# Level operands ahead of the split, and chunk pairs in the HGRN phases, in a two-layer hybrid trunk

## The chip, the cores and the metric

The kernel runs on one core of a Trainium2 chip. The metric is the device time of one execution in microseconds (us); lower is better. TensorE (PE) multiplies, VectorE (DVE) and ScalarE (ACT) prepare its operands, SyncE (SP) issues the weight loads. Each engine works its own queue in order and waits on semaphores.

## The reference

```python
def hgrn2_mixer(xn, w_in, lb, out_gain, w_out):
    q, fr, v, g = jnp.split(xn @ w_in, 4, axis=-1)            # 2048 columns each
    q = silu(q) * 128 ** -0.5
    f = lb + (1 - lb) * sigmoid(fr); k = 1 - f
    o = chunked_gated_recurrence(heads(q), heads(k), heads(v), heads(log(f)))
    return (rms_norm(o, out_gain) * silu(g)) @ w_out

def conv_glu_ffn(xn, w_up, conv_w, w_down):
    gate, val = jnp.split(causal_dwconv(xn @ w_up, conv_w), 2, axis=-1)
    return (silu(gate) * val) @ w_down

h = h + hgrn2_mixer(rms_norm(h, ..), ..);       h = h + conv_glu_ffn(rms_norm(h, ..), ..)
h = h + short_conv_mixer(rms_norm(h, ..), ..);  h = h + conv_glu_ffn(rms_norm(h, ..), ..)
return rms_norm(h, final_norm)
```

The sequence has 256 tokens, the model 2048 features, the HGRN mixer 16 heads of 128, the feed-forward part 5632 features. All is float32.

## The kernel before

**Chunks.** All weights are streamed once, in 816 chunks of 512 KB, through a ring of four slots (RING). Of each float32 operand two parts are kept, a high part in the type of the fast matmul and the low rest, and a product is made of high times high, high times low and low times high. For every chunk ACT copies the weights to their high part (`hi_ready`, L324), DVE subtracts to get the low part (`lo_ready`, the split, L537), and PE does 8 matmuls of 512 columns with the high part (`feature_highs`, L1035, "highs", H below) and 8 of 256 columns with the low part (`feature_lows`, L1045, "lows", L). PE adds to `hi_used` after the highs and to `lo_used` after the lows. ACT refills a slot's high part after `hi_used` of the chunk that was in it, and DVE's split for chunk c+4, which stands in DVE's step for chunk c, waits for `lo_used` of chunk c. SP loads raw weights once the split of the slot's last chunk is done.

**Phases.** HGRN_IN has 4 blocks (i) of 4 heads, each with 4 groups (g) of 8 chunks: forget gate, q, v (g = V_GROUP = 2) and output gate. HGRN_OUT is the output projection of the mixer, 32 chunks. Then follow UP0, DOWN0, SC_IN, SC_OUT, UP1 and DOWN1. In group 2 the roles are turned: `token_boths` (512 columns, both parts of the weights, L1058) comes first and needs `lo_ready` too, and `token_highs` (L1067) comes second and frees the high part. `run` in PE's `phase_of` says how many chunks' highs go before their lows: 1 in HGRN_IN, HGRN_OUT and DOWN1 (H L H L), RUN = 2 elsewhere (H H L L, a pair).

**Levels.** The recurrence of four heads is worked out over 128 tokens at a time by levels 1, 2, 4, ..., 128 (LEVELS). Counted from the start of group 2, n is the number of the chunk (0 to 15 in groups 2 and 3). PLAN says after which chunk's PE work a stage is issued: the diagonal (m = -1) after n = 2, levels m = 0 to 7 after 3, 5, 6, 8, 10, 12, 13 and 15, and the output stage (twelve matmuls, L1175) after 18, which is chunk 2 of the next block's first group, or of HGRN_OUT. A level stage is four matmuls of 128 columns (L1196, eight in the trace); it reads `ql` and `kl`, which DVE's `level_operands` writes two chunks ahead, into buffer m % 2, and writes `side`, of which there are two (STAGES). DVE then merges `side` into `a_diag` (`take_stage`, a copy under a mask, L806) and adds to `stage_free`, without which PE doesn't start the stage after the next. `prefixes` (L786) updates the running products between two levels.

**DVE's order in a step.** In `phase_of` of DVE a step is: `ahead` (here `last_take`), the split, the correction of a finished half group (`corrected`, L570 or L565), then `hgrn`: take of the stage after n - 1, `prefixes`, the work of `output_steps` for the block before, `level_operands`. A level's take has no wait of its own: the split of its step waits for `lo_used` of chunk n, which PE gives after the stage.

**The output of a block.** `output_steps` of DVE, step 2: the gate product (L829), the copy of the output stage (L797), the gain (L833, four); step 3, behind the split of that step: the high and low part of `act` (L838, L840), which adds to `act_ready`. In HGRN_OUT the chunks of the first group come in the order (part, k) = (0,0) (0,1) (1,0) (0,2) (1,1) (0,3) (1,2) (1,3), and the first chunk with a new k waits for `act_ready` of block k. The last block's `act` is made in HGRN_OUT itself, in steps 2 and 3, and chunk 5, (0,3), is the first that needs it. After chunk 6 comes a stage that sums squares (L1027), for which DVE waits in the same step (`rms`).

Below, o0 to o31 are the chunks of HGRN_OUT, v0 to v7 those of group 2 of a block; H(o5) is the 8 highs of o5, L(o5) its lows, "the split for o6" the DVE operation that makes its low part.

Of the kernel before, what the change touches and what calls it, by code (L numbers as in the profile page):

```python
# [44 lines left out]
RUN = 2  # L45
LEVELS = [1, 2, 4, 8, 16, 32, 64, 128]
# [36 lines left out]
HGRN_IN = Phase(None, 4, 4, DT, scales=3)  # L83
HGRN_OUT = Phase(HGRN_IN, 2, 2, DT)
# [24 lines left out]
LEAD = 2  # L109
# [21 lines left out]
def trunk(nc, x, parameters, hgrn_w_in, hgrn_w_out, sc_w_in, sc_w_out, ffn_w_up, ffn_w_down, final_norm, identity,  # L131
          level_masks, out):
    with ExitStack() as ctx:
# [3 lines left out]
        def sem(name):  # L137
            return ctx.enter_context(nc.semaphore(name))
# [70 lines left out]
        scaled_ready = sem("scaled_ready")  # L209
        stage_done = sem("stage_done")  # L210
        stage_free = sem("stage_free")
        inits = sem("inits")
        chain = sem("chain")
        late_chain = sem("late_chain")
# [36 lines left out]
        def at(i, per, first):  # L251

            return i * per + first
# [238 lines left out]
        def _(dve):  # L492
# [287 lines left out]
            def prefixes(i, m):  # L780

                n = LEVELS[m]
                pre = halves(fpre[:], n)
                shape = [P, TG * T // (2 * n), n]
                await_mark(i)
                mark(v.tensor_tensor(pre[:, :, 1], pre[:, :, 1], pre[:, :, 0, n - 1:n].to_broadcast(shape), ALU.mult))  # L786
# [67 lines left out]
            def hgrn(i, first, g, kk):  # L854
                n = g * HGRN_IN.cpg + kk - 2 * HGRN_IN.cpg
                if first and (g, kk) == (0, X_LATE_AT):
                    input_low_parts(X_LATE)
                    lower_bound()
                if first and (g, kk) == (0, BOUND_AT):
                    lower_bound_rest()  # L860
                if first and g == 0 and kk in SQUARES_AT:
                    n_sq = SQUARES_AT.index(kk)
                    dve.wait_ge(sq_ready, n_sq + 1)
                    src = [ta, tb][n_sq % 2]
                    then(v.tensor_tensor(sq_acc[:], sq_acc[:], src[:, 0:2, :], ALU.add))
                    then(v.tensor_tensor(sq_acc[:], sq_acc[:], src[:, 2:4, :], ALU.add))
                    if n_sq == DT // TG - 1:
                        then(v.tensor_copy(sq_mirror[:], mirrored(sq_acc[:, :, P:])))
                    v.sem_inc(sq_sum, 1)
                if first and (g, kk) == (0, last):  # L870
                    rms(0, S_RS_HGRN, T + 2)
                for stage, (after, _, _) in enumerate(PLAN):
                    if n == after + 1:
                        take_stage(i, stage)
                if kk == last and g != V_GROUP:
                    scaled(i, HGRN_IN, g, min(g, V_GROUP), ta[:])
                if first and (g, kk) == (1, 0):
                    dve.wait_ge(inits, 4)
                    dve.wait_ge(masks_loaded, 16)
                    dve.wait_ge(conv_par_loaded, 16)  # L880
                if (g, kk) == (1, 0):

                    dve.wait_ge(gate_sig, at(i, 3, 1))
                    for j in range(TG):
                        c = bass.ds(i * TG + j, 1)
                        o = v.tensor_scalar(fpre[:, j, :], tb[:, j, :], one_less_lb[:, c], lb[:, c], ALU.mult, ALU.add)
                    link(o, i)
                    v.tensor_scalar(kh[:], fpre[:], -1.0, 1.0, ALU.mult, ALU.add)
                    v.tensor_scalar(kl[:, 1], mirrored(fpre[:, :, P:]), -1.0, 1.0, ALU.mult, ALU.add)
                for after, what, m in PLAN:  # L890
                    if what == LEVEL and 0 <= m < len(LEVELS) - 1 and n == after - LEAD + 1:
                        prefixes(i, m)
                if not first:
                    output_steps(i - 1, g, kk)
                if n == 0:

                    dve.wait_ge(gate_sig, at(i, 3, 2))
                    v.scalar_tensor_tensor(out=qh[:], in0=ta[:], scalar=float(P) ** -0.5, in1=tb[:],
                                           op0=ALU.mult, op1=ALU.mult).then_inc(qk_ready, 1)
                    dve.wait_ge(qk_ready, at(i, 1 + len(LEVELS), 1))  # L900
                for after, what, m in PLAN:
                    if what == LEVEL and m >= 0 and n == after - LEAD:
                        level_operands(i, m)

            phase_of(HGRN_IN, hgrn, ahead=last_take, into=lambda g: ta)
            late[0] += 4 * HGRN_IN.n
            carried.append(lambda g, kk: output_steps(HGRN_IN.n - 1, g, kk))
            residual_phase(HGRN_OUT, 0, 8, NORM_FFN, 1, S_RS_OUT)
# [95 lines left out]
        def _(pe):  # L1004
# [94 lines left out]
            def phase_of(phase, src, ready, ready0, per=1, rs=None, pieces=None, carry=None, rs_at=(0, RS_AT)):  # L1099

                def between(i, first, g, kk):
                    if carry and first:
                        carry(g, kk)
                    if first and rs and (g, kk) == rs_at:
                        sum_squares(*rs)
                    if pieces:
                        pieces(i, first, g, kk)

                def body(i, first):
                    for g in range(phase.groups):  # L1110
                        seen = 0
                        steps = phase.steps(first, g)
                        run = 1 if phase in (HGRN_IN, HGRN_OUT, DOWN1) else RUN
                        ends_here = phase is DOWN1 and i == DOWN1.n - 1 and g == DOWN1.groups - 1
                        for k0 in range(0, phase.cpg - RING * ends_here, run):
                            chunks = []
                            for kk in range(k0, k0 + run):
                                part, k, begin, end = steps[kk]
                                c = phase.c0 + g * phase.cpg + kk
                                a = g * phase.parts + part  # L1120
                                if begin:

                                    pe.wait_ge(acc_free, at(i, phase.api, phase.a0 + a + 1))
                                need = k + 1 if phase.parts == 2 else k * KC // TG + 1
                                if first and g == 0 and need > seen:
                                    pe.wait_ge(ready, ready0 + need * per)
                                    seen = need
                                pe.wait_ge(hi_ready, at(i, phase.cpi, c + 1))
                                to = acc[:, a % SETS]
                                if phase is DOWN1:  # L1130
                                    pe.wait_ge(lo_ready, at(i, phase.cpi, c + 1 + RING))
                                    low, high = wide_tokens(to, c, src, k, begin, end)
                                    low.then_inc(lo_used, 1)
                                    high.then_inc(hi_used, 1)
                                elif phase is HGRN_IN and g == V_GROUP:
                                    if first and part == 0:
                                        pe.wait_ge(mirror_ready, k + 1)
                                    pe.wait_ge(lo_ready, at(i, phase.cpi, c + 1 + RING))
                                    token_boths(to, c, src, k, begin)
                                else:  # L1140
                                    feature_highs(to, c, src, k, begin)
                                chunks.append((c, to, k, end))
                            if phase is DOWN1:
                                between(i, first, g, k0)
                                continue
                            for kk in range(k0, k0 + run - 1):
                                between(i, first, g, kk)
                            for c, to, k, end in chunks:
                                if phase is HGRN_IN and g == V_GROUP:
                                    token_highs(to, c, src, k, end)  # L1150
                                else:
                                    pe.wait_ge(lo_ready, at(i, phase.cpi, c + 1 + RING))
                                    feature_lows(to, c, src, k, end)
                            between(i, first, g, k0 + run - 1)
                        if ends_here:
                            last_chunks(acc[:, g % SETS], CHUNKS - RING, src, steps[-RING:])
                loop(pe, phase, body)
# [88 lines left out]
```

## Time and profile before

| | |
|---|---|
| median of 3 runs | 2348.74 us (2348.08 to 2348.83) |
| the profiled execution | 2348.23 us |
| its span, first to last instruction | 2346.4 us |
| granted TensorE clock, mean | 0.999 of full speed |
| PE busy | 2326.7 us (99%) |
| DVE busy | 1698.7 us (72%) |
| ACT busy | 1047.0 us (45%) |
| DMA | 434.91 MB, 185 GB/s |

The kernel before is bound by TensorE from 9.10 us to 2338.7 us. Busy time of matmuls overlaps in the records, so that the time of a stretch is read from the starts of its rows. HGRN_IN ends at 418.10 us, HGRN_OUT at 512.04 us.

### The profile page before, as it was taken

The page shows a single profiled execution, that of the slowest core. Times are in us where ns is not written, and L with a number is a line of the kernel's source. Part 1 is how long each engine was busy: PE and PEld are TensorE (multiplying, and loading weights), DVE is VectorE, ACT ScalarE, POOL GpSimd, SP SyncE. Part 2 cuts the span into 40 slices and gives each one's busy share as a digit, 9 for nine tenths or more (in the row PEclk, how much of TensorE's full clock was granted, in tenths as well). Part 3 has the DMA queues.
Part 4 walks back from the last instruction along what each step waited for, and adds up shares of the span by engine and source line. Part 5 has one row for each costly group of instructions (what it writes and reads, how often), then busy time and mean ns, then how long its engine had stood idle before and what let it go on. Part 6 is the DMA issues. An engine that isn't in the chain of part 4 may idle for free.

```text
span 2346.4 us, 37237 instructions
## 1 busy us (share of the span) xinstructions
PE 2326.7 (99%) x13180; PEld 2045.2 (87%) x13180; DVE 1698.7 (72%) x2151; ACT 1047.0 (45%) x1146; POOL 2.7 (0%) x8
## 2 busy tenths in 40 slices
PE   8999999999999999999999999999999999999998
PEld 7888888888888888888888888888888888888887
DVE  7979788778788878865555666666788788785444
ACT  6443444454444444444444444444444444443443
POOL 0000000000000000000000000000000000000000
PEclk9999999999999999999999999999999999999999
DMA  7555555556666566566555666565656656665664
GB/s 245 160 171 153 170 164 167 170 179 190 188 187 190 185 188 188 187 196 190 189 187 187 192 188 189 180 197 179 198 180 192 194 179 195 188 206 185 192 192 157
DMA packets 410283, 434.91 MB, mean 185 GB/s; under 512 B 13264, under 2 KB 386384, under 8 KB 410064
## 3 DMA queue, kind: packets, MB, share of 16 engines
q1 hardware_dynamic: 409616, 431.53, 58.9%
q10 hardware_dynamic: 576, 2.16, 0.3%
q8 instruction: 58, 0.95, 0.2%
q14 instruction: 33, 0.27, 0.0%
HBM read 431.54 MB, written 2.10 MB: 185 GB/s over the span
## 4 chain that ended last, share of the span: by engine, by line
PE 97%; DVE 2%; issue 1%; ACT 0%; DMA 0%; DVEq 0%; ACTq 0%
PE acc L1035 54%; PE acc L1045 28%; PE acc L1081 3%; PE acc L1082 3%; PE acc L1080 3%; PE acc L1058 2%; PE side L1196 1%; PE acc L1067 1%; PE side L1175 0%; PE side L1191 0%; DVE kl L769 0%; DVE a_diag L806 0%; DVE a_diag L800 0%; DMA par<-in_parameters 0%; PE side L1027 0%
## 5 line engine op out<-in xcount | busy, mean ns | idle before, releaser
L537 DVE TENSOR_TENSOR w_parts<-raw,w_parts 128x1024 fp32r<-128x1024 f32 x816 | 982.5, 1223 | 575.9 <-PE acc L1045 347.9
L324 ACT ACTIVATE w_parts<-raw 128x1024 fp32r<-128x1024 f32 x816 | 859.3, 1060 | 1023.3 <-PE acc L1035 804.5
L1035 PE MATMUL acc<-xn,w_parts 128*128 128x512 f32 x4352 | 1051.1, 392 | 9.1 <-DVE xn L595 9.1
L1035 PEld LDWEIGHTS acc<-xn,w_parts 128*128 128x128 f32 x4352 | 797.6, 189 | 161.6 <-issue 9.1
L1045 PEld LDWEIGHTS acc<-xn,w_parts 128*128 128x128 f32 x4352 | 565.1, 191 | 25.2
L1045 PE MATMUL acc<-xn,w_parts 128*128 128x256 f32 x4352 | 573.2, 283 | 0.0
L1035 PE MATMUL acc<-act,w_parts 128*128 128x512 f32 x1216 | 293.6, 391 | 0.7 <-DVE act L840 0.7
L1035 PEld LDWEIGHTS acc<-act,w_parts 128*128 128x128 f32 x1216 | 222.5, 188 | 43.3 <-DVE act L840 0.9
L1045 PEld LDWEIGHTS acc<-act,w_parts 128*128 128x128 f32 x1216 | 158.0, 191 | 7.2
L1045 PE MATMUL acc<-act,w_parts 128*128 128x256 f32 x1216 | 160.2, 283 | 0.0
L1080 PE MATMUL acc<-w_parts,act 128*128 128x512 f32 x352 | 137.3, 390 | 0.0
L1082 PE MATMUL acc<-w_parts,act 128*128 128x512 f32 x352 | 137.0, 389 | 0.0
L1081 PE MATMUL acc<-w_parts,act 128*128 128x512 f32 x352 | 137.0, 389 | 0.0
L338 ACT ACTIVATE corr<-acc 128x512 f32<-128x512 f32 x144 | 85.7, 595 | 76.0 <-PE acc L1045 76.0
L619 DVE SCALAR_TENSOR_TENSOR tb<-pad,par,tb 128x256 f32<-128x256 f32 x208 | 90.9, 482 | 12.2 <-DVE tb L617 0.3
L619 DVE SCALAR_TENSOR_TENSOR ta<-pad,par,ta 128x256 f32<-128x256 f32 x176 | 77.5, 482 | 11.9
L1082 PEld LDWEIGHTS acc<-w_parts,act 128*128 128x128 f32 x352 | 66.1, 188 | 13.7
L1080 PEld LDWEIGHTS acc<-w_parts,act 128*128 128x128 f32 x352 | 66.1, 188 | 13.6
L1081 PEld LDWEIGHTS acc<-w_parts,act 128*128 128x128 f32 x352 | 66.1, 188 | 13.5
L570 DVE TENSOR_TENSOR pad<-acc,corr 128x512 f32<-128x512 f32 x96 | 65.6, 684 | 0.0
L367 ACT ACTIVATE xn<-h,par 128x256 fp32r<-128x256 f32 x64 | 28.7, 501 | 77.0 <-DVE h L657 59.8
L399 ACT ACTIVATE ta<-ta 128x1024 f32<-128x1024 f32 x22 | 23.4, 1065 | 82.7 <-DVE ta L619 82.7
(123 smaller groups left out, 1014.9 us busy)
## 6 DMA issues: line engine op xcount, KB each, us to landing
raw<-in_ffn_w_up SPq DMA_DIRECT2D x352, 512.0 KB, 3.6
raw<-in_ffn_w_down SPq DMA_DIRECT2D x176, 512.0 KB, 4.6
raw<-in_hgrn_w_in SPq DMA_DIRECT2D x128, 512.0 KB, 3.7
raw<-in_sc_w_in SPq DMA_DIRECT2D x96, 512.0 KB, 4.6
raw<-in_hgrn_w_out SPq DMA_DIRECT2D x32, 512.0 KB, 3.9
raw<-in_sc_w_out SPq DMA_DIRECT2D x32, 512.0 KB, 4.4
h<-in_x SPq DMA_DIRECT2D x4, 512.0 KB, 7.5
final_w<-in_final_norm ACTq DMA_DIRECT2D x1, 1024.0 KB, 7.0
```

What stands on the lines that cost most here:

```text
L324: nc.scalar.activation(w_parts[:, c % RING, :, 0, :], raw[:, c % RING], ACT.Copy).then_inc(hi_ready, 1)
L338: o = nc.scalar.activation(corr[:], acc[:, a % SETS, :, T:], ACT.Copy)
L367: o = nc.scalar.activation(xn[:, bass.ds(tile + j, 1), 0, :], h[:, bass.ds(tile + j, 1), :], ACT.Copy, scale=par[:, bass.ds(weight + tile ...
L537: v.tensor_tensor(w_parts[:, c % RING, :, 1, :], raw[:, c % RING], w_parts[:, c % RING, :, 0, :].bitcast(F32), ALU.subtract).then_inc(lo_r ...
L570: o = v.tensor_tensor(dst[:, part * TW:(part + 1) * TW, :], acc[:, a % SETS, :, 0:T], corr[:], ALU.add)
L619: o = v.scalar_tensor_tensor(out=dst[:, j, :], in0=src, scalar=w, in1=dst[:, j, :], op0=ALU.mult, op1=ALU.add)
L1035: o = mm(to[:, j, :], w[:, q, 0, j * P:(j + 1) * P], src[:, k * KW + q, :, :].rearrange("p n t -> p (n t)"), start=begin and q == 0, stop= ...
L1045: o = mm(to[:, j, T:], w[:, q, 1, j * P:(j + 1) * P], src[:, k * KW + q, 0, :], start=False, stop=end and q == KW - 1, skip_group_check=True)
L1058: o = mm(to[:, b, :], x_block(src, k * KW + q, 0, b), w[:, q].rearrange("p n d -> p (n d)"), start=begin and q == 0, stop=False, skip_grou ...
L1080: mm(bank, x_hi, hi, start=begin and q == 0, stop=False)
L1081: low = mm(bank, x_hi, lo, start=False, stop=False)
L1082: high = mm(bank, x_lo, hi, start=False, stop=end and q == KC - 1)
```

## The change

Two things are changed. In HGRN_IN and HGRN_OUT `run` becomes RUN, so that these 160 chunks go in 80 pairs; a stage that follows an even chunk is then issued between the highs and the lows of its pair, one that follows an odd chunk after the pair. And DVE's level work (prefixes, level operands, take) moves from behind the split of its step to ahead of it (`levels`), with the operands ahead of the take; a step that takes a stage waits for `stage_done` of that stage first and adds to a new semaphore, `stage_seen`, for which nobody waits. The work of `output_steps` stays behind the split.

```diff
             def levels(i, g, kk):
+                last_take(i, g, kk)
+                n = g * HGRN_IN.cpg + kk - 2 * HGRN_IN.cpg
+                done = [stage for stage, (after, what, _) in enumerate(PLAN) if what == LEVEL and n == after + 1]
+                for stage in done:
+                    dve.wait_ge(stage_done, at(i, HGRN_STAGES, S_HGRN + stage + 1))
+                    v.sem_inc(stage_seen, 1)
+                for after, what, m in PLAN:
+                    if what == LEVEL and 0 <= m < len(LEVELS) - 1 and n == after - LEAD + 1:
+                        prefixes(i, m)
                 for after, what, m in PLAN:
                     if what == LEVEL and m >= 0 and n == after - LEAD:
                         level_operands(i, m)
+                for stage in done:
+                    take_stage(i, stage)
...
-                for stage, (after, _, _) in enumerate(PLAN):
-                    if n == after + 1:
-                        take_stage(i, stage)
...
-                for after, what, m in PLAN:
-                    if what == LEVEL and 0 <= m < len(LEVELS) - 1 and n == after - LEAD + 1:
-                        prefixes(i, m)
...
-            phase_of(HGRN_IN, hgrn, ahead=last_take, into=lambda g: ta)
+            phase_of(HGRN_IN, hgrn, ahead=levels, into=lambda g: ta)
...
-                        run = 1 if phase in (HGRN_IN, HGRN_OUT, DOWN1) else RUN
+                        run = 1 if phase is DOWN1 else RUN
```

Lines after the change are numbered one higher in DVE's part (the split is L538) and nine higher in PE's (highs L1044, lows L1054, the output stage L1184).

**Place 1, DVE in a block of the heads, step n = 4.** From the split of the step before the change (level 0 taken, prefixes of level 1, operands of level 2) to the next split:

```order
L537 TENSOR_TENSOR w_parts<-raw,w_parts 128x4x256 [waits lo_used,hi_ready]
L806 COPY_PREDICATED a_diag<-masks,side 128x512
L508 REGISTER_ALU
L786 TENSOR_TENSOR fpre<-fpre 128x256x2 [waits chain]
L508 REGISTER_ALU
L760 TENSOR_TENSOR ql<-qh,fpre 128x512 [waits chain]
L769 TENSOR_TENSOR kl<-kh,suf 128x64x4 x2
L775 REGISTER_ALU
L777 TENSOR_TENSOR suf<-suf,fpre 128x128x4 [waits qk_ready]
```

The same step after the change:

```order
L509 REGISTER_ALU [waits stage_done]
L787 TENSOR_TENSOR fpre<-fpre 128x256x2 [waits chain]
L509 REGISTER_ALU
L761 TENSOR_TENSOR ql<-qh,fpre 128x512 [waits chain]
L770 TENSOR_TENSOR kl<-kh,suf 128x64x4 x2
L776 REGISTER_ALU
L778 TENSOR_TENSOR suf<-suf,fpre 128x128x4 [waits qk_ready]
L807 COPY_PREDICATED a_diag<-masks,side 128x512
L536 REGISTER_ALU
L538 TENSOR_TENSOR w_parts<-raw,w_parts 128x4x256 [waits lo_used,hi_ready]
```

The split has moved from the first row to the last, and the take from ahead of the operands to behind them.

**Place 2, PE in HGRN_OUT, from o2 into the output stage.** Before the change the stage stands behind the lows of o2:

```order
L1035 MATMUL acc<-act,w_parts 128x512 [waits hi_ready,acc_free]
L1035 MATMUL acc<-act,w_parts 128x512 x7
L1045 MATMUL acc<-act,w_parts 128x256 [waits lo_ready]
L1045 MATMUL acc<-act,w_parts 128x256 x7
L1175 MATMUL side<-a_diag,vt 128x128 [waits stage_free,acc_free]
```

After the change it stands behind the highs of o2 and o3:

```order
L1044 MATMUL acc<-act,w_parts 128x512 [waits hi_ready,acc_free]
L1044 MATMUL acc<-act,w_parts 128x512 x7
L1044 MATMUL acc<-act,w_parts 128x512 [waits hi_ready,act_ready]
L1044 MATMUL acc<-act,w_parts 128x512 x7
L1184 MATMUL side<-a_diag,vt 128x128 [waits stage_free,acc_free]
```

The lows of o2, which release DVE's split in its step 2, have gone from ahead of the stage to behind it.

**Place 3, DVE in HGRN_OUT, steps 2 and 3, after the change.** The first row is the splits of steps 1 and 2 (for o5 and o6), the fifth that of step 3:

```order
L538 TENSOR_TENSOR w_parts<-raw,w_parts 128x4x256 [waits lo_used,hi_ready] x2
L830 TENSOR_TENSOR tb<-ta,tb 128x1024 [waits gate_sig]
L798 COPY o_sb<-side 128x1024 [waits stage_done,late_chain]
L834 SCALAR_TENSOR_TENSOR tb<-o_sb,par,tb 128x256 [waits stage_free]
L834 SCALAR_TENSOR_TENSOR tb<-o_sb,par,tb 128x256 x3
L538 TENSOR_TENSOR w_parts<-raw,w_parts 128x4x256 [waits lo_used,hi_ready,late_chain]
L839 CAST act<-tb 128x4x256
L841 TENSOR_TENSOR act<-tb,act 128x4x256 [waits late_chain]
```

Nothing has moved in this queue; it reads the same before the change, one line number lower.

**Place 4, PE in HGRN_OUT behind the output stage.** Before the change, from the highs of o4 to the first of o5:

```order
L1035 MATMUL acc<-act,w_parts 128x512 [waits hi_ready]
L1035 MATMUL acc<-act,w_parts 128x512 x7
L1045 MATMUL acc<-act,w_parts 128x256 [waits lo_ready]
L1045 MATMUL acc<-act,w_parts 128x256 x7
L1035 MATMUL acc<-act,w_parts 128x512 [waits hi_ready,act_ready]
```

After the change, the pair of o4 and o5:

```order
L1044 MATMUL acc<-act,w_parts 128x512 [waits hi_ready]
L1044 MATMUL acc<-act,w_parts 128x512 x7
L1044 MATMUL acc<-act,w_parts 128x512 [waits hi_ready,act_ready]
L1044 MATMUL acc<-act,w_parts 128x512 x7
L1054 MATMUL acc<-act,w_parts 128x256 [waits lo_ready]
```

The wait for `act_ready` of the last block now comes before the lows of o4.

## Rows read from the trace of the kernel before

**Rows 1.** The page, part 1: busy us (share of the span) and instructions.

```profile
PE 2326.7 (99%) x13180; PEld 2045.2 (87%) x13180; DVE 1698.7 (72%) x2151; ACT 1047.0 (45%) x1146; POOL 2.7 (0%) x8
```

**Rows 2.** Timeline of PE, single chunks, HGRN_OUT: start us, duration us, what.

```profile
445.00 2.00 PE L1035 MATMUL acc<-act,w_parts 128*128 128x512 f32 x8
...
509.24 2.00 PE L1035 MATMUL acc<-act,w_parts 128*128 128x512 f32 x8
```

**Rows 3.** Chain that ended last, pairs in UP0: start us, us, what.

```profile
535.33 3.65 PE acc L1035 x16
...
1064.17 3.65 PE acc L1035 x16
```

**Rows 4.** Timeline of PE, second block, v5 to v7 and two level stages.

```profile
178.38 0.28 PE L1067 MATMUL acc<-w_parts,xn 128*128 128x256 f32 x1
...
180.15 0.47 PE L1058 MATMUL acc<-w_parts,xn 128*128 128x512 f32 x1
...
182.08 0.28 PE L1067 MATMUL acc<-w_parts,xn 128*128 128x256 f32 x1
...
184.68 0.48 PE L1058 MATMUL acc<-w_parts,xn 128*128 128x512 f32 x1
```

**Rows 5.** Who waited for whom: us in total, times, longest us.

```profile
PE side L1196 <- DVE kl L769: 2.3, 4, 0.6
```

**Rows 6.** Timeline of DVE, second block, steps 3 and 4; idle in brackets.

```profile
174.14 1.23 DVE L537 TENSOR_TENSOR w_parts<-raw,w_parts 128x1024 fp32r<-128x1024 f32 x1 [2.59 <-ACT w_parts L324]
...
182.89 0.75 DVE L769 TENSOR_TENSOR kl<-kh,suf 128x256 f32<-128x256 f32 x2
```

**Rows 7.** Timeline of PE in HGRN_OUT: H(o2), output stage, H(o3), H(o4), H(o5), H(o6).

```profile
423.78 2.00 PE L1035 MATMUL acc<-act,w_parts 128*128 128x512 f32 x8
...
426.57 0.39 PE L1175 MATMUL side<-a_diag,vt 128*128 128x128 f32 x2
...
429.17 2.09 PE L1035 MATMUL acc<-act,w_parts 128*128 128x512 f32 x8
...
432.05 2.00 PE L1035 MATMUL acc<-act,w_parts 128*128 128x512 f32 x8
...
435.65 2.11 PE L1035 MATMUL acc<-act,w_parts 128*128 128x512 f32 x8 [0.65 <-DVE act L840]
...
438.55 2.00 PE L1035 MATMUL acc<-act,w_parts 128*128 128x512 f32 x8
```

**Rows 8.** Timeline of DVE in HGRN_OUT, steps 2 and 3.

```profile
426.97 1.23 DVE L537 TENSOR_TENSOR w_parts<-raw,w_parts 128x1024 fp32r<-128x1024 f32 x1 [1.57 <-ACT w_parts L324]
428.11 1.22 DVE L829 TENSOR_TENSOR tb<-ta,tb 128x1024 f32<-128x1024 f32 x1
429.52 1.22 DVE L797 COPY o_sb<-side 128x1024 f32<-128x1024 f32 x1 [0.19 <-PE side L1175]
...
432.51 1.22 DVE L537 TENSOR_TENSOR w_parts<-raw,w_parts 128x1024 fp32r<-128x1024 f32 x1
...
434.37 1.23 DVE L840 TENSOR_TENSOR act<-tb,act 128x1024 fp32r<-128x1024 f32 x1
```

**Rows 9.** Timeline of ACT in HGRN_OUT: the high parts for o12 to o15.

```profile
452.58 3.96 ACT L324 ACTIVATE w_parts<-raw 128x1024 fp32r<-128x1024 f32 x4
```

**Rows 10.** Timeline of PE, UP0: a pair with a squares stage between highs and lows.

```profile
528.74 3.83 PE L1035 MATMUL acc<-xn,w_parts 128*128 128x512 f32 x16
...
535.17 3.82 PE L1035 MATMUL acc<-xn,w_parts 128*128 128x512 f32 x16
```

**Rows 11.** Timeline of PE, the first two chunks of the kernel.

```profile
9.10 3.75 PE L1035 MATMUL acc<-xn,w_parts 128*128 128x512 f32 x8 [9.10 <-DVE xn L595]
...
14.29 2.01 PE L1035 MATMUL acc<-xn,w_parts 128*128 128x512 f32 x8
```

**Rows 12.** Windows at the end: busy PE, PEld, DVE, ACT, POOL, granted clock, DMA share, GB/s.

```profile
2338.00:2340.00 2.00, 0.74 (x4) 0.28 (x2) 0.69 (x1) 0.50 (x1) 0.00 (x0) 1.00 1.02 401
...
2342.00:2344.00 2.00, 0.00 (x0) 0.00 (x0) 0.04 (x1) 0.10 (x1) 0.00 (x0) 0.52 0.55 225
```

More of the change, by code:

```diff
@@ L211, in trunk @@
         stage_free = sem("stage_free")
+        stage_seen = sem("stage_seen")
         inits = sem("inits")
@@ L900, in hgrn, with levels @@
                     dve.wait_ge(qk_ready, at(i, 1 + len(LEVELS), 1))
+            def levels(i, g, kk):
+                last_take(i, g, kk)
[7 more added lines that the diff above has]
+                        prefixes(i, m)
                 for after, what, m in PLAN:
```

## Prediction

> **What bounds the kernel now.** I read the busy times first: PE is busy for 2326.7 of 2346.4 us, DVE for 1698.7 [rows 1]. The change can only pay where PE waits or where its own order costs time, and it does harm only where it makes PE wait. So I went on to the waits of PE, then to its timeline around each of them, and last to DVE's and ACT's timelines, to see who is late and by how much. Inside the two HGRN phases PE waits at two kinds of place. In every block of heads the stage of level 2 waits for `kl` from DVE, four times [rows 5]. And in HGRN_OUT H(o5) waits 0.65 us for the last block's `act` [rows 7].
>
> **Pairs.** From H(o8) at 445.00 to H(o31) at 509.24 PE does 23 single chunks, so one takes 2.793 us [rows 2]. In UP0 95 pairs lie between 535.33 and 1064.17, so a pair takes 5.567 us [rows 3]. A pair saves 2 x 2.793 - 5.567 = 0.019 us; 80 pairs save **1.5 us**. A chunk's highs take 1.84 and its lows 0.95 us; a pair's highs take 3.66.
>
> What pairs do to the stages: a stage after an even chunk now stands between highs and lows, 0.87 us later than before (3.66 against 2.79 from the start of the pair). Does it cost more there? In UP0 a pair with a squares stage in its middle takes 535.17 - 528.74 = 6.43 us, 0.86 over a plain pair [rows 10]; the same stage between single chunks takes 445.00 - 438.55 = 6.45 against 5.59, again 0.86 [rows 2, 7]. So the position costs nothing; for the 24 stages of the heads and outputs that move I take 0, with bounds of 0.05 us each to either side, 1.2 us in all.
>
> **Level operands.** In the second block the lows of v5 start at 178.38 and the next highs, one level stage later, at 180.15, in 1.77 us; from the lows of v6 to H(v7), with the stage of level 2, it is 184.68 - 182.08 = 2.60 [rows 4]. The wait costs 0.83 us, in four blocks **3.3 us**. Will it go? Before, DVE sits idle for 2.59 us until 174.14, when ACT's high part lets it split for v7, and `kl` of level 2 is ready at 182.89 + 0.75 = 183.64 [rows 6], 9.5 us later. Counted back from 178.38 (H 1.84, or 1.93 behind a stage, L 0.95, stage 0.81), H(v3) began at 169.97. With pairs H(v3) goes ahead of the diagonal stage, so the lows of v2, which in group 2 free the high part that ACT refills, start 0.89 later than they ended, at 170.86, and end at 171.8. ACT then needs 0.2 us to notice and 1.05, the split 1.14: DVE is free for step 3 at 174.2, as before. From there the queue to `kl` of level 2 is the same 9.5 us without one split (1.14) and one take (1.11), which now stand behind it: 7.25 us, ready at 181.45. PE wants the stage at 183.03 + 0.87 = 183.9. So the wait goes, with 2.4 us to spare. What is late next is the take of level 0, without which `side` isn't free for that stage: 181.45 + 0.61 + 1.11 = 183.2, 0.7 us early. Carried on step by step with the same durations the later stages are met with 0.8 us (level 6) to 2.9 us. The splits, now behind the level work, are up to 3 us later: that for v7 is done 8.7 + 4.4 = 13.1 us after H(v2), and PE needs it at 16.5. The new `stage_done` waits end when the stage does, which lies before DVE gets there in each step. All of that is covered by PE's ring of four.
>
> **The output of the last block.** This is where the change costs. Before, the split for o6 (DVE step 2) starts at 426.97, the gate product at 428.11, the copy of the output at 429.52, the split of step 3 at 432.51 and L840 at 434.37; it ends at 435.60, and H(o5) starts at 435.65 instead of 433.89 + 0.95 = 434.84 [rows 7, 8]. In that chain the split for o6 needed only L(o2), which PE had done ahead of the output stage. With pairs (place 2) PE does H(o2) from 423.78, H(o3) from 425.62, the output stage from 427.43, which takes 429.17 - 426.57 = 2.60 us, and L(o2) only from 430.03 to 431.1. DVE notices at 431.3. Its queue hasn't changed (place 3): the gate product, which needs nothing new, and the copy of an output that was done at 430 both stand behind the split. From the start of that split to the end of L840 are 435.60 - 426.97 = 8.63 us of back-to-back work, so `act_ready` comes at 431.3 + 8.63 = 439.9 and H(o5) starts at 440.0. And H(o5) is now wanted earlier (place 4), at 432.05 + 1.84 = 433.9. PE stands still for 6.1 us, where it stood 0.8. From H(o5) to the end of the pair are 0.1 (the first matmul after a wait), 1.84 and 1.91 us: H(o6) starts at 443.85 where it started at 438.55. That is **+5.3 us**, and none of it is given back, since from there on PE is never waiting.
>
> In the three other blocks the same chain runs 4.3 us later too, but there nobody needs `act` yet; the splits of steps 2 to 4 come with 4 us to spare.
>
> **Behind it in HGRN_OUT.** The squares stage after o6 also moves into its pair, so DVE's split for o10, which waits for L(o6), starts 5.7 us after H(o6), and `rms` and all that follows it is 2.5 us later against PE. ACT's high part for o12 began at 452.58 [rows 9] and took 1.05, for a start of H(o12) at 445.00 + 4 x 2.79 = 456.17: 2.5 us early. That reserve is used up exactly. I take 0, and 0 to 0.6 us for the range.
>
> **The clock.** At the end of the kernel the last matmul ends at 2338.74, the window up to 2344 shows a clock of 0.52, and the windows before 2342 show 1.00 [rows 12]: the grant falls to the lower of its two levels (1.2 of 2.4 GHz) some 3.3 us after the last matmul. At the beginning the first two chunks take 14.29 - 9.10 = 5.19 us instead of 2.79 [rows 11], at the lower level. A gap of about 6 us at H(o5) is longer than 3.3, so the clock probably falls in it, and the restart costs up to 5.19 - 2.79 = **2.4 us** as at the beginning (1.2 to 3.2 for the range). The Trainium skill, "TensorE: Matmul & The Clock Gate", section "Why this matters for your kernels", warns against idle gaps between bursts of matmuls, since the engine is then throttled again; by it the time is that of A, and the trace's tail agrees with it.
>
> **The sum**, against the profiled execution (2348.23 us, of which 2346.4 are span): -1.5 - 3.3 + 5.3 + 2.4 = +2.9, so 2351.1. That execution lies 0.5 us under the median of the runs, so a median of 2348.74 + 2.9 = 2351.6; I say **2351.5**.
>
> **Rivals.** (A) The forecast: wait of 6 us and a fallen clock, 2351.5. Chance 0.60. (B) The wait is there, but the clock stays: 2348.74 + 0.5 = 2349.2. For it speaks that 6 us isn't much over 3.3 and that the row shows one fall only. Chance 0.23. (C) The last block's `act` isn't held by L(o2), and only the output stage's own 0.87 us and the earlier demand count: PE waits 1.8 us more than before, no fall of the clock, 2348.74 - 4.8 + 1.8 = 2345.7. Against it stands the order in place 3; a `lo_used` that had come earlier in another way is not to be seen. Chance 0.05. (D) Slower: the takes, which now stand behind the operands, hold back `side`. The point from which it decides is the 0.7 us of level 2's stage: if DVE reaches step 4 more than that later than I count, because of the semaphore step or of ACT's high part, PE waits for the rest in each of four blocks; at 2 us late that is 4 x 1.3 = 5.2 on top of A, 2356.7. For it: DVE works there without a gap for some 38 us per block. Against it: the work is the same and its durations are regular. Chance 0.09. (E) The operands' gain comes and the pairs leave HGRN_OUT unharmed, because DVE's chain is shorter than counted: 2348.74 - 4.8 = 2343.9. Chance 0.03.
>
> **How the numbers follow.** This kernel's measurement can tell 0.2%, 4.7 us, from no change: under 2344.0 is faster, over 2353.4 slower. A and B with their bounds (the clock 1.2 to 3.2, the position 1.2 to either side, o12 up to 0.6) reach from 2348.0 to 2354.1; together they hold 0.83, of which 0.05 lies over 2353.4. The range from 2346.5 to 2354.0 leaves out C, E, D and the edge of A. Faster 0.03, slower 0.09 + 0.05 = 0.14, the same 0.83.
>
> **What would show it.** In the profile after: no row in which L1196's counterpart in PE waits for `kl`; plain pairs in HGRN_IN at 5.57 us; a PE row in HGRN_OUT behind H(o4) with some 6 us idle, released by DVE's low part of `act`, and ahead of that a split on DVE released by PE's lows of o2; for 3 to 5 us behind the gap matmuls of 512 columns that start 0.43 instead of 0.23 us apart (A) or not (B); H(o12) without a wait. I am wrong if the gap is under 3 us (the chain isn't held as I say), or if stages in the heads wait for `stage_free` (D).

## The result and the profile after

The change makes the kernel slower by a little over a thousandth: 2351.28 us (median of 20 runs, 2350.33 to 2351.89) against 2348.18 us before (20 runs, 2348.01 to 2348.83). The ratio of after to before is 1.0013 with a 95% interval of 1.0007 to 1.0018. The profiled execution's span grew from 2346.4 to 2350.0 us, 3.6 us; the execution that was profiled after the change took 2351.83 us, 0.55 more than the median. Where rows are compared below, they are of single executions; times of whole kernels are medians.

The page of the kernel after, part 1, answers to [rows 1]:

```profile
PE 2327.7 (99%) x13180; PEld 2047.9 (87%) x13180; DVE 1695.0 (72%) x2151; ACT 1044.3 (44%) x1146; POOL 2.7 (0%) x8
```

PE's instructions are the same 13180, and of the 3.6 us only 1.0 is busy time, so the loss is time in which it stands still or runs slowly (a slow matmul counts as busy for longer). Its waits say where. Of the kernel after (engine and line, waited for; us in total, times, longest):

```profile
PE acc L1044 <- DVE xn L596: 8.8, 1, 8.8
PE acc L1044 <- DVE act L841: 5.8, 1, 5.8
```

The first is the start of the kernel. The four waits for `kl` of [rows 5] are gone. The wait of H(o5) for the last block's `act` is nine times as long as it was (5.81 against 0.65 us). PE's timeline there, after (start us, duration, what, idle before):

```profile
425.73 2.16 PE L1054 MATMUL acc<-act,w_parts 128*128 128x256 f32 x16
427.72 2.00 PE L1044 MATMUL acc<-act,w_parts 128*128 128x512 f32 x8
435.54 3.78 PE L1044 MATMUL acc<-act,w_parts 128*128 128x512 f32 x8 [5.81 <-DVE act L841]
439.12 3.22 PE L1054 MATMUL acc<-act,w_parts 128*128 128x256 f32 x16
442.18 3.80 PE L1044 MATMUL acc<-act,w_parts 128*128 128x512 f32 x16
```

The rows are L(o2) and L(o3), H(o4), H(o5), L(o4) and L(o5), and H(o6) with H(o7). DVE's timeline in the same place, after, answers to [rows 8]:

```profile
427.03 1.23 DVE L538 TENSOR_TENSOR w_parts<-raw,w_parts 128x1024 fp32r<-128x1024 f32 x1 [5.28 <-PE acc L1054]
428.18 1.22 DVE L830 TENSOR_TENSOR tb<-ta,tb 128x1024 f32<-128x1024 f32 x1
429.43 1.22 DVE L798 COPY o_sb<-side 128x1024 f32<-128x1024 f32 x1
...
434.26 1.22 DVE L841 TENSOR_TENSOR act<-tb,act 128x1024 fp32r<-128x1024 f32 x1
```

The split for o6 sat 5.28 us waiting for PE's lows and everything for `act` stood behind it. And the clock, windows of the kernel after (columns as in [rows 12]):

```profile
434.20:434.80 0.60, 0.00 (x0) 0.00 (x0) 0.56 (x2) 0.00 (x0) 0.00 (x0) 1.00 0.07 12
434.90:435.50 0.60, 0.00 (x0) 0.00 (x0) 0.58 (x1) 0.00 (x0) 0.00 (x0) 0.50 0.83 254
441.00:441.60 0.60, 0.60 (x5) 0.60 (x4) 0.47 (x1) 0.00 (x0) 0.00 (x0) 0.50 0.00 0
441.80:442.40 0.60, 0.60 (x6) 0.57 (x5) 0.60 (x2) 0.02 (x1) 0.00 (x0) 1.00 0.00 0
```

PE's last matmul ahead of the gap ends at 429.72. The grant is full until 434.86, 5.1 us later, then at the lower level (1.2 of 2.4 GHz), and full again from 441.69. H(o5) starts 0.7 us after the fall.

Where the time went, from the starts of PE's first matmul in each stretch:

| stretch | before | after | difference | forecast |
|---|---|---|---|---|
| to the first matmul | 9.10 | 8.85 | -0.25 | 0 |
| first two chunks | 7.99 | 8.51 | +0.52 | 0 |
| rest of HGRN_IN | 401.01 | 396.45 | -4.56 | -4.5 |
| o0 to o7 | 26.90 | 34.77 | +7.87 | +7.6 |
| o8 to o31 | 67.04 | 67.07 | +0.03 | -0.2 |
| the rest | 1834.40 | 1834.38 | 0.0 | 0 |

### The profile page after: what moved, and what is told of

It is laid out like the page before. It is cut to its first block, busy times and chain, and to the rows that moved or that the text cites. A ratio compares the mean times of both kernels' runs of the same rounds, so it can differ in the third digit from the quotient of the medians.

```text
span 2350.0 us, 37283 instructions
## 1 busy us (share of the span) xinstructions
PE 2327.7 (99%) x13180; PEld 2047.9 (87%) x13180; DVE 1695.0 (72%) x2151; ACT 1044.3 (44%) x1146; POOL 2.7 (0%) x8
## 4 chain that ended last, share of the span: by engine, by line
PE 99%; DVE 0%; DMA 0%; ACT 0%; issue 0%; DVEq 0%; ACTq 0%
PE acc L1044 54%; PE acc L1054 28%; PE acc L1091 3%; PE acc L1089 3%; PE acc L1090 3%; PE acc L1067 2%; PE acc L1076 1%; PE side L1205 1%; PE side L1184 0%; PE side L1200 0%; DMA par<-in_parameters 0%; PE side L1036 0%; PE side L1024 0%; DVE tb L834 0%; ACT xn L368 0%
## 5 line engine op out<-in xcount | busy, mean ns | idle before, releaser
L538 DVE TENSOR_TENSOR w_parts<-raw,w_parts 128x1024 fp32r<-128x1024 f32 x816 | 979.5, 1222 | 582.4 <-PE acc L1054 420.8
L1044 PE MATMUL acc<-xn,w_parts 128*128 128x512 f32 x4352 | 1041.8, 392 | 8.8 <-DVE xn L596 8.8
L1044 PEld LDWEIGHTS acc<-xn,w_parts 128*128 128x128 f32 x4352 | 801.9, 189 | 164.4 <-issue 8.8
L1054 PEld LDWEIGHTS acc<-xn,w_parts 128*128 128x128 f32 x4352 | 556.8, 191 | 19.9
L1054 PE MATMUL acc<-xn,w_parts 128*128 128x256 f32 x4352 | 566.4, 283 | 0.0
L1044 PE MATMUL acc<-act,w_parts 128*128 128x512 f32 x1216 | 292.2, 392 | 5.8 <-DVE act L841 5.8
L1044 PEld LDWEIGHTS acc<-act,w_parts 128*128 128x128 f32 x1216 | 224.4, 189 | 49.9 <-DVE act L841 6.2
L1054 PEld LDWEIGHTS acc<-act,w_parts 128*128 128x128 f32 x1216 | 157.1, 193 | 5.9
L1054 PE MATMUL acc<-act,w_parts 128*128 128x256 f32 x1216 | 159.1, 284 | 0.0
```

The lines of the kernel that those rows point to most:

```text
L538: v.tensor_tensor(w_parts[:, c % RING, :, 1, :], raw[:, c % RING], w_parts[:, c % RING, :, 0, :].bitcast(F32), ALU.subtract).then_inc(lo_r ...
L1044: o = mm(to[:, j, :], w[:, q, 0, j * P:(j + 1) * P], src[:, k * KW + q, :, :].rearrange("p n t -> p (n t)"), start=begin and q == 0, stop= ...
L1054: o = mm(to[:, j, T:], w[:, q, 1, j * P:(j + 1) * P], src[:, k * KW + q, 0, :], start=False, stop=end and q == KW - 1, skip_group_check=True)
```

## Experiments

All times below are medians of 10 or 11 runs (of 4 for e3); the kernel before was measured beside each set and gave 2348.2 to 2348.3 us. The expectations took their pieces from the profiled execution of the change and put them under its median of 2351.3, while that execution lay 0.55 us over the median; the measured times of e1, e4, e6, e7 and e8 are 0.4 to 0.7 us over the expected ones.

**e1: pairs in the heads only.**

```diff
-                        run = 1 if phase is DOWN1 else RUN
+                        run = 1 if phase in (HGRN_OUT, DOWN1) else RUN
```

> The changed kernel with single chunks again in HGRN_OUT; the heads keep pairs and the new order. My theory: all of the loss lies in HGRN_OUT, which took 93.94 us before and 101.84 after, so this gives 2351.3 - 7.9 = 2343.4 us, and H(o5) waits 0.65 us for act as before. Rival: the new order in the heads itself makes the last block's act late; then H(o5) waits for over 2 us here too and the time is over 2345.

Measured: 2343.83 us, ratio to before 0.9981 (0.9971 to 0.9991). HGRN_OUT took 93.93 us, as in the kernel before, and H(o5) waited 0.7. The loss lies in HGRN_OUT alone; the rival is out.

**e2: DVE's new order alone.**

```diff
-                        run = 1 if phase is DOWN1 else RUN
+                        run = 1 if phase in (HGRN_IN, HGRN_OUT, DOWN1) else RUN
```

> The new order of DVE alone, single chunks everywhere. My theory: the order takes away the four waits of 0.83 us for kl of level 2, so 2348.2 - 3.3 = 2344.9 us. Rival: the waits went because pairs put that stage 0.87 us later; then they are still here and the time is 2348.2.

Measured: 2344.96 us, ratio 0.9986 (0.9976 to 0.9996), 3.3 us less than before. No level stage waits. With single chunks the order is enough for the 3.3 us.

**e3: pairs alone.** To the kernel before, pairs and, since a take can no longer lean on its split, a wait (the line that creates `stage_seen` is left out):

```diff
                     if n == after + 1:
+                        dve.wait_ge(stage_done, at(i, HGRN_STAGES, S_HGRN + stage + 1))
+                        v.sem_inc(stage_seen, 1)
                         take_stage(i, stage)
...
-                        run = 1 if phase in (HGRN_IN, HGRN_OUT, DOWN1) else RUN
+                        run = 1 if phase is DOWN1 else RUN
```

> Pairs alone: the kernel before with pairs in HGRN_IN and HGRN_OUT, DVE's level work behind the split as before, with a wait for stage_done before each take. By my sum kl of level 2 is ready 9.5 us after DVE is free at 174.2, at 183.7, and the stage is wanted 0.87 us later than before, at 183.9: the wait goes here too, by 0.2 us, and the time is 2351.3. Rival: the order is needed; the four waits of 0.83 stay and the time is 2354.6.

Measured: 2360.46 us, ratio 1.0051 (1.0034 to 1.0068). Theory and rival (2351.3 and 2354.6) were both far too low. PE's waits and its timeline in the second block, e3:

```profile
PE side L1199 <- DVE kl L770: 5.1, 12, 0.8
```

```profile
185.44 1.15 PE L1199 MATMUL side<-ql,kl 128*128 128x128 f32 x8 [0.19 <-DVE kl L770]
192.44 1.15 PE L1199 MATMUL side<-ql,kl 128*128 128x128 f32 x8 [0.29 <-DVE kl L770]
...
209.24 1.15 PE L1199 MATMUL side<-ql,kl 128*128 128x128 f32 x8 [0.82 <-DVE kl L770]
```

Three stages per block have rows of a wait now, those of levels 2, 3 and 6, instead of one, and that of level 1 starts 0.2 us late (at 180.44, where the lows ahead of it would have let it start at 180.24). Part of what I had left out is in DVE's rows of e3:

```profile
174.09 1.23 DVE L538 TENSOR_TENSOR w_parts<-raw,w_parts 128x1024 fp32r<-128x1024 f32 x1 [1.74 <-ACT w_parts L325]
175.23 0.69 DVE L787 TENSOR_TENSOR fpre<-fpre 128x512 f32<-128x512 f32 x1
175.84 1.22 DVE L538 TENSOR_TENSOR w_parts<-raw,w_parts 128x1024 fp32r<-128x1024 f32 x1
...
184.56 0.76 DVE L770 TENSOR_TENSOR kl<-kh,suf 128x256 f32<-128x256 f32 x2
```

The operation that waits until 174.09 is the split for v6, not for v7: pairs hold back the lows of v2. The 9.5 us that I took from [rows 6] begin with the split for v7, so they start at 175.84, and `kl` of level 2 is ready at 185.32, which is 9.5 later. My expectation let them begin at the end of the split for v6; the prefix of 175.23 stands between, 0.61 us. Counted from H(v2) (165.47 before, 166.41 in e3), `kl` came after 18.91 us, where 183.7 - 165.47 = 18.23 were expected. That explains the wait of level 2, which is the shortest of the three. I had looked at no other stage. Ahead of level 3's operands DVE stands for 0.90 us until ScalarE's high part is there (its split at 188.67), which it didn't in the kernel before; why level 6 waits longest I haven't traced. In all, HGRN_IN took 413.9 us from its first matmul, 4.9 more than before the change. With pairs the new order is worth 9.2 us (e3 against the change), without them 3.3.

**e4: o2 and o3 singly**, so that L(o2) is ahead of the output stage; all else as changed.

```diff
-                        for k0 in range(0, phase.cpg - RING * ends_here, run):
+                        own = first and g == 0 and phase is HGRN_OUT
+                        for k0, run in ([(0, 2), (2, 1), (3, 1), (4, 2), (6, 2)] if own else
+                                        [(k, run) for k in range(0, phase.cpg - RING * ends_here, run)]):
```

> The changed kernel, but in HGRN_OUT's first group o2 and o3 go singly, so L(o2) is ahead of the output stage; o4 and o5 stay a pair. My theory: act comes when it came before, 1.7 us after H(o5) is wanted; of the wait of 5.97 us 4.2 go, and with them the 3.0 us of the fallen clock: 2351.3 - 7.2 = 2344.1. Rival: the earlier demand of H(o5) in its pair is what counts; then over 4 us of wait remain and the time is over 2348.

Measured: 2344.76 us, ratio 0.9985 (0.9975 to 0.9994). PE, e4, H(o4) and H(o5):

```profile
427.62 2.00 PE L1044 MATMUL acc<-act,w_parts 128*128 128x512 f32 x8
431.22 2.11 PE L1044 MATMUL acc<-act,w_parts 128*128 128x512 f32 x8 [1.60 <-DVE act L841]
```

The wait is 1.76 us from start to start (431.22 - 427.62 - 1.84), the highs behind it run at full speed (the granted clock is 1.00 from 431 to 433), and o0 to o7 take 27.8 instead of 34.8 us. So 4.2 of the 6 us come from the pair of o2 and o3, and with them goes the fallen clock. This run takes away two things at once: the lows of o2 are no longer held, and the output stage ends 0.86 us earlier after H(o0) (11.06 against 11.92 us). DVE's copy now waits 0.19 us for the stage, so by an estimate up to 0.9 of the 4.2 us need the earlier stage too. e7 leaves the stage where the change has it.

**e5: o4 and o5 singly**, the list in e4 now `[(0, 2), (2, 2), (4, 1), (5, 1), (6, 2)]`: L(o4) is done ahead of the wait.

> The changed kernel, but o4 and o5 go singly: L(o4) is done ahead of the wait, o2 and o3 stay a pair. My theory: act comes as late as in the changed kernel, H(o5) is wanted 0.95 us later, so the wait is 5.0 us: 2351.3 - 0.95 = 2350.3 if the clock falls in it, 2347.4 if it doesn't. In the changed kernel it fell 5.1 us after the last matmul's end, at the end of the kernel before 3.3 us after it, so I give each half. Rival: the demand counts most; a wait under 2 us and 2344.

Measured: 2349.82 us, ratio 1.0006 (0.9997 to 1.0016). H(o5) waits and is slow, e5:

```profile
429.60 1.11 PE L1054 MATMUL acc<-act,w_parts 128*128 128x256 f32 x8
435.58 3.78 PE L1044 MATMUL acc<-act,w_parts 128*128 128x512 f32 x8 [4.87 <-DVE act L841]
```

The clock fell in this gap too, and early in it: L(o4) ends at 430.71, and the grant falls at 433.14, 2.4 us later. Windows of e5:

```profile
432.50:433.00 0.50, 0.00 (x0) 0.00 (x0) 0.50 (x1) 0.23 (x1) 0.00 (x0) 1.00 0.00 0
433.20:433.40 0.20, 0.00 (x0) 0.00 (x0) 0.20 (x1) 0.00 (x0) 0.00 (x0) 0.50 0.00 0
```

From H(o0) to H(o8) are 33.06 us, 1.7 less than in the change. Of these 1.0 are the shorter wait (5.0 against 6.0), which is what the earlier demand of H(o5) is worth; the rest is that less work fell into the low level, which here began earlier in the gap and ended at 439.97:

```profile
440.00:444.00 4.00, 4.00 (x22) 3.39 (x21) 1.83 (x2) 2.52 (x4) 0.00 (x0) 1.00 0.18 54
```

**e6: the gap filled.** In front of the wait of H(o5), 22 matmuls whose result nobody reads, and a wait that guards their buffer:

```diff
+                                if phase is HGRN_OUT and first and (g, kk) == (0, 5):
+                                    pe.wait_ge(stage_free, S_RS_OUT + 1)
+                                    for n in range(22):
+                                        mm(side[:, S_RS_OUT % STAGES, 0:2 * T], src[:, 0, 0, 0:P],
+                                           src[:, 0, :, :].rearrange("p n t -> p (n t)"), start=True, stop=True,
+                                           skip_group_check=True)
```

> The changed kernel with 22 needless matmuls of 512 columns (5.0 us) between H(o4) and the wait for act, into a side buffer that nobody reads before it is written anew. My theory: the clock stays at its higher level, H(o5) starts when it did, and the 2.9 us that the slow matmuls behind the gap cost go: 2348.4. Rival: the slow restart isn't the clock, or costs nothing in the end: 2351.3.

Measured: 2348.97 us, 2.3 us less than the change with more matmuls in it. PE, e6:

```profile
429.24 5.15 PE L1137 MATMUL side<-act 128*128 128x512 f32 x22
435.21 2.12 PE L1044 MATMUL acc<-act,w_parts 128*128 128x512 f32 x8 [0.83 <-DVE act L841]
```

H(o5) starts as long after H(o4) as in the change (7.81 against 7.82 us) and takes 2.12 instead of 3.78. From H(o0) to H(o8) are 32.02 us against 34.77, 2.75 less. Apart from the matmuls put in, nothing in the stretch differs but the level of the clock, which is full here:

```profile
435.00:440.00 5.00, 4.79 (x28) 4.28 (x29) 1.77 (x3) 1.66 (x2) 0.00 (x0) 1.00 0.24 84
```

So 2.75 us are the price of the fall between these two executions, and 2.3 between the medians.

**e7: DVE's output work ahead of the split.** Gate product, copy, gain and both parts of `act` in one piece ahead of the split of step 2, the take of level 7 ahead of that of step 0, in the heads as in HGRN_OUT:

```diff
+            def output_ahead(i, g, kk):
+                if (g, kk) == (0, 0):
+                    dve.wait_ge(stage_done, at(i, HGRN_STAGES, S_HGRN + HGRN_STAGES - 1))
+                    v.sem_inc(stage_seen, 1)
+                if (g, kk) != (0, 3):
+                    output_steps(i, g, kk)
+                if (g, kk) == (0, 2):
+                    output_steps(i, g, 3)
...
```

Left out are the old call of `output_steps` behind the split, which goes, and the new calls of `output_ahead` from `levels` and in HGRN_OUT.

> The changed kernel with DVE's output work (gate product, copy of the output, gain, act's two parts) ahead of the split of step 2, the take of level 7 ahead of the split of step 0. My theory: the chain to act no longer waits for L(o2) and loses a split: act at 431.0, wanted 429.6, a wait of 1.4 us and no fall of the clock: 2351.3 - 4.6 - 3.0 = 2343.7. Rival: the chain isn't held by the split but by the output stage or ScalarE; 2351.3.

Measured: 2344.41 us, ratio 0.9984 (0.9974 to 0.9993). DVE in e7:

```profile
425.69 1.23 DVE L798 COPY o_sb<-side 128x1024 f32<-128x1024 f32 x1 [3.79 <-PE side L1194]
426.95 1.67 DVE L834 SCALAR_TENSOR_TENSOR tb<-o_sb,par,tb 128x256 f32<-128x256 f32 x4
428.66 0.69 DVE L839 CAST act<-tb 128x1024 fp32r<-128x1024 f32 x1
429.38 1.23 DVE L841 TENSOR_TENSOR act<-tb,act 128x1024 fp32r<-128x1024 f32 x1
```

The copy now waits for the output stage itself and `act` is there 4.9 us after it; H(o5) waits 1.33 us. The output stage is where the change has it and the lows of o2 are still held; only DVE's order is different. So it is the place of the output work behind the split that turns held lows into a wait.

**e8: the output stage earlier too**, behind the pair of chunks 0 and 1.

```diff
-                if (g, kk) != (0, 2):
+                if (g, kk) != (0, 1):
```

> As e7, and the output stage after chunk 1 instead of after the highs of 2 and 3. My theory: the stage ends some 3.6 us earlier, act is there before H(o5) is wanted, PE waits nowhere in HGRN_OUT: 2343.7 - 1.4 = 2342.3. Rival: the stage now waits for the take of level 7, or the splits of the next chunks come too late, in each of four blocks; 2343.7 or more.

Measured: 2342.88 us, ratio 0.9977 (0.9968 to 0.9986), the fastest together with e9: 5.3 us under before, 8.4 under the change. PE waits for no `act` and no `kl`:

```profile
PE acc L1054 <- DVE xn L596: 9.0, 1, 9.0
```

**e9: e8 with the squares stage after o5.**

```diff
-            phase_of(HGRN_OUT, act, act_ready, 0, 1, (1, S_RS_OUT), carry=lambda g, kk: output(HGRN_IN.n - 1, g, kk))
+            phase_of(HGRN_OUT, act, act_ready, 0, 1, (1, S_RS_OUT), carry=lambda g, kk: output(HGRN_IN.n - 1, g, kk),
+                     rs_at=(0, 5))
```

> As e8, with the squares stage of HGRN_OUT after o5, behind its pair, instead of in the middle of the pair of o6 and o7. In e8 the 12 pairs from H(o8) to the end of HGRN_OUT took 67.08 us, where 12 pairs at 5.567 take 66.80: by my theory H(o12) waits 0.2 to 0.3 us for ScalarE's high part, because DVE's split for o10 waits for L(o6) behind the stage. Then it goes here: 66.8 us for the 12 pairs, 2342.88 - 0.3 = 2342.6 in all. Rival: pairs of HGRN_OUT cost that much everywhere; 67.08 stays.

Measured: 2342.89 us, ratio 0.9978 (0.9969 to 0.9987), and o8 to o31 still take 67.07 us. Both the time and the 66.8 us that I had expected are missed, and the expectation was ill made: without the stage in its pair L(o6) comes 0.7 us earlier after H(o6), but so does the demand of H(o12). In the rows H(o12) starts 12.28 us after the end of L(o6) in the change (459.91 against 446.49 + 0.19 + 0.95), 12.28 in e8 and 12.28 in e9, 0.2 us later than PE's own work between them. The chain that I had described can be followed in the rows: DVE's split for o10 starts 0.26 us after L(o6), `rms`, the residual and ACT's work follow without a longer pause than 0.5 us, and ACT's high part for o12, 1.05 us from 458.71 on in the change, ends 0.15 us before H(o12) starts (0.14 in e8 and e9). But PE's row names no releaser, and no run took the chain away: I leave it argued.

## Why the prediction was right

**What bounds the kernel, and the position of stages.** Right: PE's busy time grew by 1.0 us only, and the stretches add up. Block for block HGRN_IN gained 1.13 us (the starts of blocks 2, 3 and HGRN_OUT are 2.03, 3.16 and 4.29 us earlier than before), against 0.83 for the wait and 0.31 for 16 pairs. Nothing is left over for the stages between highs and lows.

**Level operands.** Right to a tenth. The second block's v2 starts 1.06 us earlier than before. DVE should be free for step 3 at 174.2, thus 173.14, and finish `kl` of level 2 at 181.45, thus 180.4; the rows of the kernel after:

```profile
173.24 0.68 DVE L761 TENSOR_TENSOR ql<-qh,fpre 128x512 f32<-128x512 f32 x1
...
179.67 0.75 DVE L770 TENSOR_TENSOR kl<-kh,suf 128x256 f32<-128x256 f32 x2
```

They end at 180.42, and PE started the stage at 182.81, with no idle before it. My count was right for the new order. Carried over to the old order, in the expectation of e3, it left out one prefix (0.61 us) at level 2, and all other stages.

**The output of the last block.** This was the term that decided, and each link came as counted. All shifted by the 4.3 us that HGRN_IN gained, the split for o6 was forecast for 427.0 (427.03), the end of L840 for 435.6 (435.48), the gap from the demand of H(o5) for 6.1 (435.54 - 427.72 - 1.84 = 5.98). e4 and e7 took the cause away in two ways, and most of the wait went in both (1.76 and 1.49 us are left from start to start, of 5.98).

**The clock.** It fell, as in (A). The pair with H(o5) took 442.18 - 435.54 = 6.64 us instead of 3.86: 2.8 us, where the sum had 2.4 from the kernel's start. e6 puts it at 2.75. That the term was so near is in part luck, for the price isn't fixed. By the same count it was 2.4 us in e3 (451.21 - 444.96 against 3.86) and 2.0 in e5 (440.48 - 435.58 against 2.90), and at the kernel's start it was 1.6 (e9) to 2.9 us (the change) in the profiled executions. The 3.3 us from the end of the kernel before were one value of many too: the grant fell 2.1 us (e6) to 4.7 us (e1) after the last matmul of a kernel. The wait of 6 us was longer than all of them.

**Behind it.** The reserve at H(o12) wasn't just used up, it was overdrawn: PE started H(o12) 0.19 us late and its first matmuls cost 0.08 more, which eats what the 12 pairs save. It was inside the 0 to 0.6 that the text allowed, and explains why o8 to o31 gained nothing.

**The start.** Not forecast: in the profiled execution of the change the first pair ran for longer at the low speed, for 0.5 us. This term is not the change's: the first two chunks, as the same pair, took 7.21 us (e9) to 8.51 us (the change). The prediction calls its 5.19 us those of the first two chunks; they are of the first alone [rows 11], and the two took 7.99 instead of 5.59, so that the 2.4 us are the same. And the low level there is read from the distance of the matmuls, 0.44 us instead of 0.23: the clock column shows 1.00 at the start of every run, since the trace's record of the clock only begins at 12.3 to 15.1 us, where the matmuls become fast. A fast start is partly given back: where the ninth chunk begins PE waited for DVE in the traces of e4, e5 and e9, in e9 the longest:

```profile
33.62 3.93 PE L1054 MATMUL acc<-xn,w_parts 128*128 128x512 f32 x16 [0.66 <-DVE ta L571]
```

From the first matmul to this chunk are 24.72 us in e9 and 25.21 in the change, so of the 1.3 us between their first pairs 0.5 are left.

**The number.** The sum had +2.9 us; measured are 3.1 between the medians and 3.6 between the profiled executions. In the latter the clock cost 0.4 more than the sum has, the start 0.3, o8 to o31 0.2, and the gap 0.1 less. The start and the price of the fall differ from trace to trace by 0.5 us and more, so the 0.2 us between sum and medians are in part luck. The median of 3 runs that the forecast started from lies 0.56 us over that of 20; the differences are the better comparison.

**The rivals.** (B) is out by the clock in the windows, (C) and (E) by the 5.28 us in front of the split, (D) by the missing waits of the level stages. How little DVE may be late in the heads is shown by e3, in which `kl` of level 2 was ready 18.91 us after H(v2) instead of 16.01 in the change, and three stages per block waited. Those waits are for `kl`, though; the link that (D) names, a take that holds back `side`, shows in no wait of PE, neither in the change nor in e3.

## What to carry to other kernels

When a producer's chunks are issued in pairs, the release of the first chunk moves behind whatever stands in the middle of the pair; look for every queue that waits for that release and has something urgent behind it, here an `act` behind a split. Work that another engine needs soon belongs ahead of an operation that only keeps a ring full, and the ring's reserve tells how late the latter may come. If such a wait grows past some microseconds on TensorE (here 4.9 and more), add the price of its slow restart, here 2.0 to 2.8 us.

## What the runs showed of the hardware

The price of a gap depends on its length by more than the gap. Waits of PE of 0.7, 1.3 and 1.6 us (e1, e7, e4) left the clock at its full level. It fell in all three longer ones, of 4.9 us (e5), 5.8 us (the change) and 6.2 us (e3), and the slow matmuls behind them cost 2.0, 2.8 and 2.4 us more: the longest gap wasn't the dearest.

What orders the prices is how much work fell into the low level. That level lasted 6.8 us each time (433.1 to 440.0 in e5, 434.9 to 441.7 in the change, 443.4 to 450.3 in e3), but PE worked in it for 4.4, 6.1 and 5.3 us, from its restart to the rise. From these numbers I estimate 0.45 us lost for each microsecond of work in it; all three give that.

And the fall isn't tied to one idle time. Inside the kernels it came 2.4 us (e5), 4.7 us (e3) and 5.1 us (the change) after the last matmul's end, at their ends 2.1 us (e6) to 4.7 us (e1) after it. So a gap of less than 4.9 us may be enough, but no run here has one between 1.6 and 4.9 us. The window that the prediction's 3.3 us rest on, before, and two at the end of e8, whose last matmul ends at 2333.73 and whose clock falls at 2336.15:

```profile
2340.00:2342.00 2.00, 0.00 (x0) 0.00 (x0) 1.43 (x4) 1.49 (x4) 0.00 (x0) 1.00 0.03 12
```

```profile
2335.00:2336.00 1.00, 0.00 (x0) 0.00 (x0) 0.45 (x3) 0.49 (x4) 0.00 (x0) 1.00 0.07 25
2336.20:2338.00 1.80, 0.00 (x0) 0.00 (x0) 0.82 (x2) 0.88 (x1) 0.00 (x0) 0.50 0.07 30
```
